# One core, two transformer blocks: 514 instead of 516 columns from the queries on, a beginning turned tile by tile, and three query blocks of a head scored in one run

## What is computed

```python
n = rms(h, norm_mix_w)                       # h = [meta, x], 528 positions
q, k, v, glu, g_att, g_conv = split(n @ w_in)
o = diff_attention(q, k, v, lam, cid)        # 8 heads, two 64-wide maps each, chunk-causal
y_att = rms(o, subln_w) * (1 - lambda_init)
u = causal_dwconv(glu[:, :C] * sigmoid(glu[:, C:]), conv_dw_w, conv_dw_b)   # 31 taps
y_conv = silu(layernorm(u)) @ w_conv_out
h = h + (sigmoid(g_att) * y_att + sigmoid(g_conv) * y_conv) @ w_out
up = causal_dwconv(rms(h) @ w_up, ffn_dw_w, ffn_dw_b)                        # 3 taps
h = h + (silu(gate) * val) @ w_down
```

## Time and profile before

| | us |
|---|---|
| median of 3 runs | 1537.29 (1536.73 to 1538.52) |
| the profiled execution | 1537.9 |
| its span | 1536.1 |

### The profile page before, as it was taken

How to read it: one execution, slowest core, us unless ns; L and a number is a source line. 1 busy time by engine, 2 the same in 40 slices (tenths; PEclk the granted TensorE clock), 3 DMA queues, 4 the chain that set the end, 5 groups by cost and what they waited for, 6 DMA issues and landing times.

```text
span 1536.1 us, 25380 instructions
## 1 busy us (share of the span) xinstructions
PE 1520.4 (99%) x9960; PEld 1362.3 (89%) x9960; DVE 1102.3 (72%) x1549; ACT 646.9 (42%) x1014; POOL 55.7 (4%) x115
## 2 busy tenths in 40 slices
PE   8999999999999999999999999999999999999998
PEld 7999999999999999999988888878888888888887
DVE  5888888888565587777765458888748887887123
ACT  5324555555643434434423345744645333333112
POOL 0000111111000000000000020000000000000000
PEclk9999999999999999999999999999999999999999
DMA  6334222232233233233232343231132333332321
GB/s 180 83 82 110 56 59 80 56 83 56 56 95 99 83 103 89 82 100 91 65 93 76 110 119 75 66 83 42 56 110 56 110 97 94 87 104 96 110 82 55
DMA packets 235358, 131.63 MB, mean 86 GB/s; under 512 B 20984, under 2 KB 228740, under 8 KB 235284
## 3 DMA queue, kind: packets, MB, share of 16 engines
q1 hardware_dynamic: 234900, 130.40, 30.2%
q0 software_dynamic: 384, 0.20, 0.0%
HBM read 128.48 MB, written 2.10 MB: 85 GB/s over the span
## 4 chain that ended last, share of the span: by engine, by line
PE 92%; DVE 5%; ACT 2%; issue 0%; DMA 0%; SPq 0%; DVEq 0%; ACTq 0%
PE psP L710 32%; PE psS L710 25%; PE psP L775 8%; PE psS L1393 4%; PE psP L1393 4%; PE psP L732 4%; PE psP L1083 3%; PE psP L1261 1%; DVE conv L2119 1%; PE psS L1261 1%; PE psP L930 1%; DVE wl L2004 1%; PE psP L841 1%; PE psS L889 1%; PE psS L1150 1%; PE psP L917 1%
## 5 line engine op out<-in xcount | busy, mean ns | idle before, releaser
L2004 DVE TENSOR_TENSOR wl<-raw,wh 128x2048 fp32r<-128x2048 f32 x124 | 284.1, 2291 | 176.8 <-ACT wh L1448 175.5
L1448 ACT ACTIVATE wh<-raw 128x2048 fp32r<-128x2048 f32 x124 | 237.0, 1912 | 209.9 <-PE psS L1393 74.3
L710 PE MATMUL psP<-xh,wh 128*128 128x258 f32 (+2 forms) x1184 | 295.5, 312 | 1.3 <-DVE wl L2004 0.5
L710 PE MATMUL psP<-xh,wl 128*128 128x258 f32 (+2 forms) x1184 | 291.7, 309 | 0.0
L710 PE MATMUL psP<-xl,wh 128*128 128x258 f32 (+2 forms) x1184 | 291.3, 309 | 0.0
L710 PE MATMUL psS<-xh,wh 128*128 128x258 f32 (+2 forms) x880 | 209.8, 305 | 0.4 <-DVE hT L2033 0.4
L710 PE MATMUL psS<-xh,wl 128*128 128x258 f32 (+2 forms) x880 | 208.5, 304 | 0.0
L710 PE MATMUL psS<-xl,wh 128*128 128x258 f32 (+2 forms) x880 | 208.0, 303 | 0.0
L710 PEld LDWEIGHTS psP<-xh,wh 128*128 128x128 f32 x1184 | 192.8, 189 | 16.4 <-issue 2.2
L710 PEld LDWEIGHTS psP<-xl,wh 128*128 128x128 f32 x1184 | 192.5, 189 | 12.0 <-issue 0.2
L710 PEld LDWEIGHTS psP<-xh,wl 128*128 128x128 f32 x1184 | 192.3, 189 | 11.9
(11 more groups left out here) (472 smaller groups left out, 2426.1 us busy)
## 6 DMA issues: line engine op xcount, KB each, us to landing
raw<-in_w_in_dram SPq DMA_DIRECT2D x74, 512.0 KB, 5.0
raw<-in_w_up_dram SPq DMA_DIRECT2D x44, 512.0 KB, 4.7
raw<-in_ffn_up_dram SPq DMA_DIRECT2D x44, 512.0 KB, 4.6
raw<-in_ffn_down_dram SPq DMA_DIRECT2D x22, 512.0 KB, 4.0
raw<-in_w_out_dram SPq DMA_DIRECT2D x16, 512.0 KB, 4.8
raw<-in_w_down_dram SPq DMA_DIRECT2D x16, 384.0 KB, 3.6
raw<-in_w_down_dram SPq DMA_DIRECT2D x16, 320.0 KB, 4.0
raw<-in_w_conv_out_dram SPq DMA_DIRECT2D x8, 512.0 KB, 4.7
```

The lines of the kernel that those rows point to most:

```text
L710: ins = mm(ps[0:rows, a, 0:nn], W[:, s, half, k, 0:rows], Y[:, k, c0 + a * nn:c0 + (a + 1) * nn], start=(k == 0 and p == 0), stop=(k == KT ...
L1448: fn(wh[:, n % 2], raw[:, n % 2], ACT.Copy).then_inc(s_hi, 1)
L2004: V.tensor_tensor(wl[:, n % 2], raw[:, n % 2], wh[:, n % 2].bitcast(f32), ALU.subtract).then_inc(s_lo, 1)
```

## The change

Three edits.

**514 columns.** HALO = 2 names the two positions that the three-tap convolution needs, so C3 = 14, T3 = 514 and H3 = 257. The two halves of such a product are now 256 and 258 wide (Q3) and lie side by side over the border of the two banks: the first fills columns 256 to 511 of the first bank, the second columns 0 to 257 of the second. `pieces` gives the matmuls their targets, `joined` gives ACT and DVE one flat row of 514, and `row` replaces `span`. The convolution rows in the feed-forward parts start at 2 instead of 4.

**The beginning.** `normed_tile(t)` transposes the groups 0 to 2 of one token tile as soon as DVE has normed it; the last tile of group 0 goes to bank 3. ACT and DVE split group 0 in two pieces, 384 columns and 128 columns. `awake` issues matmuls of ones with ones whose results aren't used: 8 after the first transpose, then 2, 3 and 4. The meta product moves behind token tile 2 on DVE, the copy of the meta rows to hT behind `first_lo(2)`; the wait for tile 1's copy moves to the second half chunk.

**The scores.** `scores(a, 2)` moves up behind `scores(a, 1)`. Blocks 0 and 1 lie in banks 0 and 1 at columns 0 and 160, block 2 in banks 2 and 3. The maxima of block 0 wait for the scores of block 1, and the exponentials of block 0 for the maxima of block 1.

```diff
-C3 = NM - 4
+HALO = 2
+C3 = NM - HALO
 T3 = T - C3
 H3 = T3 // 2
+Q3 = (256, T3 - 256)
...
+SCORE_COL = (0, 160, 0)
...
+        def joined(ps):
+            return ps[:, :, :].rearrange("p a b -> p (a b)")[:, 512 - Q3[0]:512 + Q3[1]]
+
+        def pieces(ps, nn, rows=128, banks=2):
+            if nn == H3:
+                flat = joined(ps)
+                return [(flat[0:rows, 0:Q3[0]], 0, Q3[0]), (flat[0:rows, Q3[0]:T3], Q3[0], Q3[1])]
+            return [(ps[0:rows, a, 0:nn], a * nn, nn) for a in range(banks)]
...
+        def score_rows(t):
+            o = SCORE_COL[t]
+            return scores_ps[:, 2 * (t // 2):2 * (t // 2) + 2, o:o + PW[t]]
...
                     for p, (W, Y) in enumerate(((wh, X[0]), (wh, X[1]), (wl, X[0]))):
-                        for a in range(banks):
-                            ins = mm(ps[0:rows, a, 0:nn], W[:, s, half, k, 0:rows], Y[:, k, c0 + a * nn:c0 + (a + 1) * nn],
+                        for dst, o, w in pieces(ps, nn, rows, banks):
+                            ins = mm(dst, W[:, s, half, k, 0:rows], Y[:, k, c0 + o:c0 + o + w],
...
+            def awake(count, banks):
+                for j in range(count):
+                    mm(banks[:, j % 2], ones[:], ones[:], start=True, stop=True)
+
+            def normed_tile(t):
+                pe.wait_ge(s_xn, t + 2)
+                for k in range(3):
+                    bank = scores_ps[:, 3 if k == 0 and t == TT - 1 else k, :]
+                    ins = tr(bank[:, 128 * t:128 * (t + 1)], xn[:, t, 128 * k:128 * (k + 1)], ident[:])
+                    if t == TT - 1:
+                        ins.then_inc(s_nt, 1)
+                    elif t == TT - 2 and k == 0:
+                        ins.then_inc(s_np, 1)
...
+            awake(8, scores_ps[:, 0:2, 384:512])
             pe.wait_ge(s_xin[0], 16)
             raw_tokens(0, psP[0])
...
+            normed_tile(0)
             pe.wait_ge(s_xin[1], 16)
             raw_tokens(1, psP[1])
-            pe.wait_ge(s_xn, TT + 1)
-            for k in range(3):
-                normed_tokens(k)
-            pe.wait_ge(s_hm, 2)
+            normed_tile(1)
+            awake(2, scores_ps[:, 0:3, 384:512])
+            normed_tile(2)
+            awake(3, scores_ps[:, 1:3, 384:512])
+            pe.wait_ge(s_mx, 1)
+            normed_tile(3)
+            pe.wait_ge(s_hm, 1)
+            awake(4, psP[0][:, :, 0:128])
...
                     scores(a, 0)
                     scores(a, 1)
+                    scores(a, 2)
...
                     if h < NH:
                         values(a)
-                    scores(a, 2)
                     probs(a, 0)
...
+            first_hi(0)
+            act.wait_ge(s_np, 1)
+            fn(xh[:, 0, NM:NM + 384], scores_ps[:, 0, 0:384], ACT.Copy, scale=vmix[:, 0:1]).then_inc(s_nq, 1)
             act.wait_ge(s_mx, 1)
             fn(xh[:, :, 0:NM], mw[:], ACT.Copy).then_inc(s_ms, 1)
-            first_hi(0)
+            act.wait_ge(s_nt, 1)
+            fn(xh[:, 0, NM + 384:T], scores_ps[:, 3, 384:512], ACT.Copy, scale=vmix[:, 0:1]).then_inc(s_nh, 1)
             act.wait_ge(s_xt, 2)
             fn(hT[:, :, NM + 128:NM + 256], psP[1][:].rearrange("p a (b c) -> p (a b) c", c=128), ACT.Copy).then_inc(s_hm, 1)
-            normed_hi(0)
...
             def exps(a, t):
-                act.wait_ge(s_ma, 4 * a + t + 1)
+                act.wait_ge(s_ma, 4 * a + max(t, 1) + 1)
...
             def maxima(a, t):
-                dve.wait_ge(s_qk, 4 * a + t + 1)
+                dve.wait_ge(s_qk, 4 * a + max(t, 1) + 1)
```

More of the change, by code:

```diff
@@ L730, in project_pair @@
                         for p, (W, Y) in enumerate(((wh, X[0]), (wh, X[1]), (wl, X[0]))):
-                            for a in range(banks):
-                                ins = mm(ps[0:r, a, 0:nn], W[:, s, half, k, 0:r], Y[:, k, c0 + a * nn:c0 + (a + 1) * nn],
+                            for dst, o, w in pieces(ps, nn, r, banks):
+                                ins = mm(dst, W[:, s, half, k, 0:r], Y[:, k, c0 + o:c0 + o + w],
                                          start=(k == 0 and p == 0), stop=(k == KT - 1 and p == 2))
@@ L786, in total @@
                 pe.wait_ge(s_sa, after)
-                for a in range(2):
-                    ins = mm(ps[:, a, 0:nn], ones[:], sacc[:, which, a * nn:(a + 1) * nn], start=True, stop=True)
+                for dst, o, w in pieces(ps, nn):
+                    ins = mm(dst, ones[:], sacc[:, which, o:o + w], start=True, stop=True)
                 ins.then_inc(s_sqf, 1)
@@ L838, in _ @@
                 for half in range(2):
+                    if half == 1 and k == 0:
+                        pe.wait_ge(s_hm, 2)
                     for p, (W, Y) in enumerate(((wh, xh), (wh, xl), (wl, xh))):
@@ L873, in scores @@
             def scores(a, t):
-                if a:
-                    pe.wait_ge(s_ex, 4 * a + (0, 0, 1, 3)[t])
-                elif t >= 2:
-                    pe.wait_ge(s_ex, t - 1 if t == 2 else 3)
+                if t == 3:
+                    pe.wait_ge(s_ex, 4 * a + 3)
+                elif a:
+                    pe.wait_ge(s_ex, 4 * a)
                 if t == 0:
                     pe.wait_ge(s_ea, evacuated(2 * (N_HEAD + 2 * a) + 1)[1])
-                if a and t == 1:
+                if a and t == 2:
                     pe.wait_ge(s_ea, evacuated(2 * (N_HEAD + 2 * a) + 3)[1])
@@ L887, in scores @@
                     if t < 3:
-                        bank = scores_ps[:, 2 * (t % 2) + m, :]
-                        mm(bank[:, 0:PW[t]], q, K[:, 0:PW[t]], start=True, stop=False)
+                        bank = score_rows(t)[:, m, :]
+                        mm(bank, q, K[:, 0:PW[t]], start=True, stop=False)
                         last.append(bank[:, PW[t] - 64:PW[t]])
@@ L940, in convolution_means @@
                 pe.wait_ge(s_cs, NH - 1)
-                for a in range(2):
-                    ins = mm(psP[0][:, a, 0:H3], ones[:], nf[:, 1, a * H3:(a + 1) * H3], start=True, stop=True)
+                for dst, o, w in pieces(psP[0], H3):
+                    ins = mm(dst, ones[:], nf[:, 1, o:o + w], start=True, stop=True)
                 ins.then_inc(s_lm, 1)
@@ L1618, in _ @@
                     act.wait_ge(s_lm, 1)
-                    fn(nf[:, 0, 0:T3].rearrange("p (a b) -> p a b", a=2), psP[0][:, :, 0:H3], ACT.Copy,
-                       scale=-1.0 / D).then_inc(s_lmc, 1)
+                    fn(nf[:, 0, 0:T3], joined(psP[0]), ACT.Copy, scale=-1.0 / D).then_inc(s_lmc, 1)
                 if h == NH:
@@ L2270, in _ @@
                         dve.wait_ge(s_ml, g - 1)
-                    ins = V.scalar_tensor_tensor(t.rearrange("p (a b) -> p a b", a=2), span(sgc, g, 0, H3), 1.0,
-                                                 ALLP[gi % 4][:, :, 0:H3], ALU.add, ALU.mult)
+                    ins = V.scalar_tensor_tensor(t, row(sgc, g, 0, T3), 1.0, joined(ALLP[gi % 4]), ALU.add, ALU.mult)
                     ins.then_inc(s_ed, 1)
@@ L2289, in _ @@
                     dve.wait_ge(s_mm, gi + 1)
-                    V.scalar_tensor_tensor(span(hT, k, C3, H3), ALLP[gi % 4][:, :, 0:H3], 0.5, span(hT, k, C3, H3),
+                    V.scalar_tensor_tensor(row(hT, k, C3, T3), joined(ALLP[gi % 4]), 0.5, row(hT, k, C3, T3),
                                            ALU.mult, ALU.add).then_inc(s_ed, 1)
@@ L2700, in _ @@
             lo(N_UP2 + 2)
-            own(V.memset(upr[:, :, :, 0:4], 0.0))
-            ffn(N_UP2, 1, 1, 8, 5, 4, S)
+            own(V.memset(upr[:, :, :, 0:HALO], 0.0))
+            ffn(N_UP2, 1, 1, 8, 5, HALO, S)
             for c in range(2, FG // 2):
```

53 lines of the change are left out of this document (32 added, 21 removed).

## The result

The changed kernel takes 1539.7 us (median of 20 runs, 1539.19 to 1540.2) beside 1537.3 us for the kernel before (20 runs on the same chip): ratio 1.0015, 95% interval 1.0009 to 1.0022. It is 2.4 us slower. That is less than the 0.2% (3.1 us) that the prediction took as the limit of what one measurement tells, but with 20 runs on either side the interval leaves out a ratio of 1. The forecast was 1537.8, in a range of 1534.0 to 1541.5.

The account below looks back on a forecast made before the run. The prediction took TensorE, busy for 99% of the span, as the bound. Columns -3.6, beginning -1.8 and scores +5.9 gave +0.5 us, so 1537.8 us against the median of 1537.29, in a range of 1534.0 to 1541.5.

Parts of the forecast that it names:

- The scores, +5.9: Moving the third score block loses 5.9 us: 3.9 in steady heads, 0.7 at the first head, 1.3 at the last.
- The wait at L917: Second transposes in each head can't start until ACT has copied the values, which block 2 covered before the move.
- the slot: Time from L910 to L917 in a head, forecast to shrink from 1.10 to 0.96 us only when block 2 leaves.
- A steady head: Each of heads 2 to 7 loses 0.64 us: block 2 costs 0.78 at its new place, less 0.14 saved.
- The late maxima: Block 0's maxima and exponentials start later; hidden in steady heads, costing 0.7 us at the first head, 1.3 at the last.
- The first rival: In the heads, the values' copy doesn't hold L917, so 1.4 us are gained there; total 1530.5 us; chance 0.20.
- The beginning, -1.8: At the start, early transposes and ones bring the first product to 14.55 us and k=1 to 16.4, gaining 1.8 us.
- The second rival: At the start, ones run at the lower clock and stand in the way, losing 1.5 us; total 1541.1 us; chance 0.16.
- The columns, -3.6: In products from the queries on, 514 columns for 516 save 1.8 ns on each of 2016 pairs, 3.6 us.
- the odd start in a row: Rows of the narrower products start at column 14, not 12; named as the only possible way to a loss, without size.
- the third rival: The narrower products save by the column only, 1.1 us in place of 3.6; total 1540.3 us; chance 0.18.
- the rule of the Trainium skill: Warm matmul gap of N / 2.4 plus about 2.5 ns: two columns 0.83 ns, 1.7 us in all; total 1539.7 us.

Follow-up runs that it names:

- wb: The changed kernel with the scores part alone undone (old place, banks and waits of the score blocks): 1533.3 us, ratio 0.9975 to the kernel before.
- late: wb with one thing added: maxima and exponentials of the first query block wait until the second block is scored too; 1535.8 us, ratio 0.9991.
- s_only: The kernel before with only the third score block moved, with its columns and later waits: 1542.7 us, ratio 1.0035.
- back: The changed kernel with the third score block put back between values and probabilities, shared columns and late waits kept: 1535.2 us, ratio 0.9988.
- ones8: wb with the first 8 products of ones and without the other 9: 1535.6 us, ratio 0.9990.
- q258: wb with its 514 columns cut 258 and 256 instead of 256 and 258: 1532.0 us, ratio 0.9966; measured once more, 1532.2 us.

## Why the prediction was right, and where it was not

**The scores, +5.9, measured +6.2: right by its steps.** The wait at L917 on the copy of the values is there, 0.78 us in seven heads, six of them on the path; the slot is 1.05 us where I had put 0.96 and where it was 1.10. The run of three blocks takes 2.06 us where two took 1.27, so the block costs 0.79 at its new place, against 0.78. A steady head is 0.70 us longer (changed kernel 187.41 to 354.14, five heads in 166.73; wb 163.22), against 0.64. (Six times 0.64 is 3.8; the prediction wrote 3.9.) The late maxima cost 0.65 at the first head against 0.7, and 1.19 at the last against 1.3, both isolated by late. Only the address of the last one was wrong: it did not show as a longer wait on ACT nf, which stayed at 0.4, but in the changed kernel on ACT u (0.3 to 1.4) and otok (0.4), and in late on otok (1.2), steps of the same chain before and behind nf.

**The first rival** (no wait, one entry and exit fewer per head, 0.20) is out by s_only and back: the wait is the part's own and goes when the block returns.

**The beginning, -1.8, measured -1.8 to -2.5 (-1.9 to -2.2 counted from the last token tile): right, a little small.** The first product came 0.8 us earlier than I had worked out (13.78 for 14.55) and k=1 0.7 earlier. I had the last tile normed at 12.6, and it was at 12.04. The second rival asked whether the clock rises before about 14 us: it does, in the eight transpositions that take 1.04 us where they took 1.97. But a fallen clock under the first products is a real danger, as ones8 shows, 1.2 us slower with nine ones fewer; and the ones deserve little of the credit: without any of them 0.3 us is lost, so most of the part's gain is the transposing tile by tile.

**The columns, -3.6, measured -1.7: the step that failed.** "From 258 to 256 it falls 1.8 ns: 3.6 us" took the difference between a row of 258 and a row of 256 and booked it for every pair, on the ground that the 256-wide row is "the very form that half of the products get". Two things are wrong in it. First, the price: a pair's pace fell by 1.16 ns in the mean of the 30 pieces and by 1.40 in the last 20, not by 1.8. The 256-wide row stood in another stage and had both products of a pair at 256 columns, and one such product between two of 258 did not come down as far. Second, I multiplied by all 2016 pairs, and only the 1440 in the long pieces gave anything; 1.16 x 1440 is the 1.67 us that the stretch shows. The prediction had named the odd start in a row only as a way to lose; it did not ask whether it could take a gain away. What the heads withheld was to be had, by cutting the other way round: q258 gets 1.0 us there and 0.4 in the 30 pieces (345.36 to 344.98), which brings the part to some 3 us, near the figure forecast for another reason.

So of the total, +0.5 forecast and +2.4 measured, the 1.9 us missed are in substance this one term (1.9); the beginning gained a little more and the scores lost 0.3 more than forecast, which nearly cancels. The forecast kept the right side of zero because the scores' loss, its largest term, was right. The case that came closest was the third rival (columns by the plain slope, 1540.3, given 0.18). With the rule of the Trainium skill in place of my term the text had 1539.7, which is the median measured. That is luck as far as the runs tell: its level is off here (110 ns for 120), no stretch paid its 0.83 ns a pair, and 260 columns cost no more than 258.

## What to carry to other kernels

Work that stands between a write to a buffer and the next write to the same buffer isn't idle filling, for the first result must be copied out in between: before moving such work, look which copy it covers, and take as its gain only what the slot really shrinks by, here 0.05 us of 0.90. A price per column should be read over steps of the same size as the step that the change makes, on both sides, before it is multiplied by thousands; and each group of products should be booked in the stretch where it stands.

When three parts are changed together and the total is small, take them apart before judging: here two were worth 4.2 us together and one lost 6.4.

## What the runs showed of the hardware that I had not expected

- Columns seem to count in steps of four: 96 products take 11.47 us with 256 and 258 in turn, the same with 256 and 260, and 11.53 with 258 twice. 258 is the only length off a multiple of four that was measured.
- The order of two unequal pieces matters in some stages: 5.78 us for 48 products cut 256 and 258, 5.72 cut 258 and 256, at equal pace (11.47 for 96) in the last 20 long pieces, though DVE and ACT are busy beside those too. Why is open.
- Raising TensorE's clock early and leaving a gap can be worse than not raising it: granted clock 0.50 and 0.71 under the first products with eight ones (the beginning takes 20.07 us from the last token tile on), 1.00 with seventeen (18.84) and with none (19.15).
- The granted clock in the view by windows does not show the first, slow part of a program. In the kernel before it reads 1.00 from 14 to 16 us, where the twelve products of the earlier trace rows take 2.73 us, the pace of the lower level:

```profile
14.00:16.00 2.00, 2.00 (x10) 1.68 (x9) 1.53 (x3) 1.83 (x4) 0.00 (x0) 1.00 1.08 261
```

The durations of like products tell the level there. In the windows read here the column left 1.00 only where the clock fell again after its rise, as in ones8.
